# An encoder layer with mixture of experts: small items in two halves, token tiles moved between projections, last item behind the loops

## The chip, the cores and the metric

The kernel runs on one core of a Trainium2 chip. Its time is that of one whole execution on the device, in microseconds (us). TensorE is called PE in the profile (PEld: its weight loads, PEldq: its sequencer), VectorE is DVE, ScalarE is ACT, GpSimd is POOL, and SyncE is SP, which starts most DMA transfers.

## What is computed

One encoder layer on 1024 tokens of width 1024, all in float32. RMSNorm and one projection give queries, keys, values and a pooling input; differential attention and a pooling mixer follow, then an output projection. The second part is a mixture of experts: each token goes to 4 of 32 experts. At the end stands an RMSNorm over the whole row of each token:

```python
g = xb @ w_gate[e] + b_gate[e]
u = xb @ w_up[e] + b_up[e]
g = jnp.minimum(g, SWIGLU_LIMIT)
u = jnp.clip(u, -SWIGLU_LIMIT, SWIGLU_LIMIT)
act = (u + 1.0) * (g * jax.nn.sigmoid(g * SWIGLU_ALPHA))
y = act @ w_down[e] + b_down[e]
...
x = x + moe(rmsnorm(x, norm2[l]), ...)
return rmsnorm(x, final_norm)
```

## The kernel before

**Projections.** 32 products `proj_step` (L1161), numbered n, each with 8 steps over 128 rows of the weights. The first 16 need token tiles 0 to 3, the last 16 tiles 4 to 7. A tile reaches the projections in three steps: VectorE scales it (`scale_tokens`, L811), TensorE transposes it in 8 pieces (`transposes`, L1146), VectorE moves it out of PSUM (`move_hT`, L817). Tiles 4 to 7 take these steps in a row at n = 16.

**Items.** The rows of an expert are cut into items of at most 128; an item is treated as one of 32, 64, 96 or 128 rows. With these inputs there are 47: 24 of 128, 8 of 96, 7 of 64 and 8 of 32 rows, and each 32-row item is followed by a 128-row item of the same expert. TensorE jumps to the code of the item's size (`run_item`); the four pieces of code stand one behind the other in memory (32, 128, 64, 96). The other engines run one loop body for all sizes, `Fori(0, MAX_ITEMS)` with MAX_ITEMS = 64, of which 17 turns are empty.

An item works in units of 256 of the 1024 hidden columns. Where an item has under 128 rows, column groups of TensorE's array work side by side: with 32 rows four groups take one unit's share each, so that all 1024 hidden columns are one unit (b = 0), with N = 512 (256 gate and 256 up columns) in each product. The order of a 32-row item is: half of the gate and up products (`gate_up`, L1388, k = 0 to 3), the transposes of the next item's first rows (L1325), the other half (k = 4 to 7), the index products for a later item (`index`, L1317), register loads for the next item (`next_item`, L1487 to L1490), the transposes of the next item's other rows (L1325), the bias of the down projection (L1412), the transposes of the hidden rows (L1396), and the down projection (`down_32`, L1449). Between the gate and up products and L1396, ScalarE takes the sigmoid (L739) and VectorE does three steps (L1094, L1096, L1099); between L1396 and L1449, ScalarE moves the transposed rows (L743). 64-row items have two units and the down projection `down_64` (L1435) in four parts; there the second unit's hidden rows are transposed after the second part.

SyncE loads an expert's weights in four parts as the last item of the one before frees them: gate and up rows 0 to 3 and 4 to 7 (L408), down rows 0 to 3 and 4 to 7 (L415, semaphores `s_wk[2]` and `s_wk[3]`). The last of these is issued when the item before has ended.

**The end of an item and of the kernel.** ScalarE scales the item's rows by their gates (L759), GpSimd adds them to the residual rows in DRAM in four indirect transfers (L590). After the loops SyncE waits for the last item's addition, loads all 1024 rows (L451), ScalarE squares and sums them and takes a root (L767, L769), VectorE takes the reciprocal and scales (L1118, L1122), and SyncE stores (L455).

## Time and profile before

| | us |
|---|---|
| median of 3 runs | 2294.33 (2292.27 to 2297.32) |
| the profiled execution | 2295.37 |
| its span, first to last instruction | 2293.6 |
| TensorE busy | 2184.3 (95% of the span) |
| the chain that ended last: TensorE, DMA | 92%, 4% of the span |
| projections and pooling products | 15.5 to 251.4 |
| attention and output projection | to 548.3 |
| items | 579.35 to 2258.19 |
| after the last product | to 2293.6 |

The mean granted TensorE clock is 0.981 of full speed. A line number names a line of the kernel before. A timeline row has start, length, engine, line, operation, what it writes <- what it reads, count, and in brackets how long the engine had been idle and what ended it.

### The profile page before, as it was taken

The page shows a single profiled execution, that of the slowest core. Times are in us where ns is not written, and L with a number is a line of the kernel's source. Part 1 is how long each engine was busy: PE and PEld are TensorE (multiplying, and loading weights), DVE is VectorE, ACT ScalarE, POOL GpSimd, SP SyncE. Part 2 cuts the span into 40 slices and gives each one's busy share as a digit, 9 for nine tenths or more (in the row PEclk, how much of TensorE's full clock was granted, in tenths as well). Part 3 has the DMA queues.
Part 4 walks back from the last instruction along what each step waited for, and adds up shares of the span by engine and source line. Part 5 has one row for each costly group of instructions (what it writes and reads, how often), then busy time and mean ns, then how long its engine had stood idle before and what let it go on. Part 6 is the DMA issues. An engine that isn't in the chain of part 4 may idle for free.

```text
span 2293.6 us, 29668 instructions
## 1 busy us (share of the span) xinstructions
PE 2184.3 (95%) x9773; PEld 993.1 (43%) x9774; DVE 654.2 (29%) x1931; ACT 567.1 (25%) x1162; POOL 455.9 (20%) x480
## 2 busy tenths in 40 slices
PE   8999899997899999999999999999999999999993
PEld 4444477543444344344433434434443444444441
DVE  2010599354322222221222222222122212222223
ACT  2000488311221222211122222221122211222223
POOL 1014011214121212212122121221212211222121
PEclk9999999998999999999999999999999999999997
DMA  6100300324567967858869796685889777677854
GB/s 264 37 0 0 147 1 1 101 91 157 190 206 292 369 228 239 307 173 319 313 207 365 243 337 221 229 300 179 314 311 381 273 269 292 204 240 243 311 183 165
DMA packets 148233, 499.00 MB, mean 218 GB/s; under 512 B 10058, under 2 KB 34655, under 8 KB 146623
## 3 DMA queue, kind: packets, MB, share of 16 engines
q1 hardware_dynamic: 112192, 443.12, 50.1%
q0 software_dynamic: 34128, 50.35, 10.9%
q10 hardware_dynamic: 1874, 5.02, 0.6%
q8 instruction: 24, 0.39, 0.1%
q14 instruction: 15, 0.11, 0.0%
HBM read 460.15 MB, written 42.50 MB: 219 GB/s over the span
## 4 chain that ended last, share of the span: by engine, by line
PE 92%; DMA 4%; DVE 2%; issue 1%; POOL 1%; ACT 1%; SPq 0%; ACTq 0%; DVEq 0%; POOLq 0%
PE psum L1388 42%; PE psum L1424 14%; PE psum L1161 10%; PE psum L1216 5%; PE psum L1435 4%; PE psum L1234 3%; PE psum L1205 3%; PE psum L1449 3%; PE psum L1325 2%; DMA weights<-in_w_down 2%; PE psum L1396 2%; PE psum L1382 2%; PE psum L1243 1%; DMA weights<-in_w_up 1%; DMA work<-normed_rows,work 1%
## 5 line engine op out<-in xcount | busy, mean ns | idle before, releaser
L1388 PE MATMUL psum<-weights,work 128*128 128x512 f32 (+2 forms) x3520 | 1030.7, 599 | 1.7 <-DMA weights<-in_w_up 1.7
L1388 PEld LDWEIGHTS psum<-weights,work 128*128 128x128 f32 (+2 forms) x3520 | 381.0, 153 | 486.3 <-issue 477.8
L590 POOL DMA_INDIRECT residual_rows<-work x188 | 293.1, 1559 | 456.5 <-ACT work L759 410.4
L1424 PE MATMUL psum<-weights,work 128*128 128x512 f32 x768 | 337.5, 592 | 0.0
L1001 DVE TENSOR_REDUCE work<-psum 128x8 f32 x48 | 8.8, 184 | 803.1 <-PE psum L1339 803.1
L550 POOL DMA_INDIRECT work<-normed_rows,work x49 | 50.4, 1028 | 898.8 <-DVE work L988 840.4
L1161 PE MATMUL psum<-weights 128*128 128x512 f32 x512 | 220.5, 593 | 2.6 <-DVE weights L817 2.6
L1424 PEld LDWEIGHTS psum<-weights,work 128*128 128x128 f32 x768 | 143.9, 190 | 164.4 <-issue 160.8
L725 ACT ACTIVATE work<-psum 128x512 f32<-128x512 f32 x96 | 57.8, 602 | 445.9 <-PE psum L1325 445.9
L739 ACT ACTIVATE work<-psum 128x256 f32<-128x256 f32 x188 | 71.3, 384 | 382.5 <-PE psum L1388 382.5
L759 ACT ACTIVATE work<-psum,work 128x256 f32<-128x256 f32 x188 | 73.8, 476 | 334.0 <-PE psum L1424 239.5
L1094 DVE TENSOR_SCALAR work<-psum 128x256 f32<-128x256 f32 x188 | 79.7, 424 | 254.2 <-ACT work L739 247.1
L1161 PEld LDWEIGHTS psum<-weights 128*128 128x128 f32 x512 | 97.0, 190 | 125.0 <-issue 121.9
L1216 PE MATMUL psum<-weights 128*128 128x512 f32 x256 | 113.3, 600 | 0.0
L1435 PE MATMUL psum<-weights,work 128*64 128x512 f32 x480 | 109.3, 597 | 3.3 <-ACT work L743 3.3
L743 ACT ACTIVATE work<-psum 128x256 f32<-128x256 f32 x188 | 72.8, 387 | 159.3 <-PE psum L1396 159.3
L1099 DVE SCALAR_TENSOR_TENSOR work<-work 128x256 f32<-128x256 f32 x188 | 80.0, 426 | 19.5
L863 DVE CUSTOM_DVE_ANT_0 work<-psum,weights 128x1024 f32<-128x1024 f32 x64 | 78.4, 1225 | 12.0 <-PE psum L1205 11.9
L643 ACT ACTIVATE work<-work,negmax 128x1024 f32<-128x1024 f32 x64 | 73.3, 1145 | 31.0 <-DVE negmax L867 30.9
L1096 DVE TENSOR_TENSOR work<-psum,work 128x256 f32<-128x256 f32 x188 | 78.0, 415 | 0.0
L1396 PEld LDWEIGHTS psum<-ident,work 128*128 128x128 f32 x284 | 36.3, 141 | 91.0 <-issue 81.7
L1449 PE MATMUL psum<-weights,work 128*32 128x256 f32 x1024 | 65.3, 410 | 8.7 <-ACT work L743 4.4
(194 smaller groups left out, 1553.6 us busy)
## 6 DMA issues: line engine op xcount, KB each, us to landing
weights<-in_w_gate SPq DMA_DIRECT2D x64, 2048.0 KB, 7.9
weights<-in_w_up SPq DMA_DIRECT2D x64, 2048.0 KB, 13.7
weights<-in_w_down SPq DMA_DIRECT2D x64, 2048.0 KB, 11.4
weights<-in_w_in SPq DMA_DIRECT2D x8, 1024.0 KB, 16.4
residual_rows<-x SPq DMA_DIRECT2D x9, 512.0 KB, 3.8
normed_rows<-work ACTq DMA_DIRECT2D x9, 512.0 KB, 3.9
x<-in_x SPq DMA_DIRECT2D x8, 512.0 KB, 9.5
bias_rows_repeated<-bias_rows SPq DMA_DIRECT2D x4, 1024.0 KB, 10.2
```

The costliest lines, as they stand in the source:

```text
L590: pl.indirect_dma_start(acc_d[:, :], bass.IndirectOffsetOnAxis(dest[:, b:b + 1], 0), yrow[:, b * BLK:(b + 1) * BLK], None, compute_op=ALU. ...
L863: dve.tensor_tensor_reduce(out=prob[:, u % SETS, m, :], in0=PS[:, 2 * m * HALF:(2 * m + 2) * HALF], in1=bias[:, h, at:at + SEQ], scale=1.0 ...
L1094: dve.tensor_scalar(ucl[:, b, :], bank(b, BLK, BLK), LIMIT + 1.0, 1.0 - LIMIT, ALU.min, ALU.max).then_inc(s_ucl, 1)
L1096: dve.tensor_tensor(gact[:, b, :], bank(b, BLK), sig[:, b, :], ALU.mult).then_inc(s_sg, 1)
L1099: dve.scalar_tensor_tensor(hid[:, b, :], gact[:, b, :], ACT_LIMIT, ucl[:, b, :], ALU.min, ALU.mult).then_inc(s_hid, 1)
L1161: return pe.matmul(bank(4 + n % 4), lhs, rhs, start=(k == 0), stop=(k == DT - 1))
L1216: mm = pe.matmul(bank(n % 4), mixT[:, c, i * P:(i + 1) * P], w_out[:, c, q * HALF:(q + 1) * HALF], start=(c == 0), stop=(c == DT - 1))
L1388: mm = pe.matmul(out.rearrange("p (m n) -> p m n", m=2), xT[:, k, lo:lo + cols], wgu[:, :, k, blk * BLK:(blk + 1) * BLK], start=False, sto ...
L1396: mm = pe.transpose(bank(6, P, s * P), hid[:, b, s * P:(s + 1) * P], ident[:, :])
L1424: mm = pe.matmul(bank(4 + h), actT[:, k, :], wdn[:, k, h * HALF:(h + 1) * HALF], start=False, stop=(k == DT - 1))
L1435: mm = pe.matmul(PS[64 * h:64 * h + 64, 4 * HALF:5 * HALF], actT[:, 2 * b + s, 64 * c:64 * c + 64], wdn[:, k, h * HALF:(h + 1) * HALF], st ...
L1449: mm = pe.matmul(PS[32 * h:32 * h + 32, at:at + BLK], actT[:, 2 * b + s, 32 * c:32 * c + 32], wdn[:, k, h * BLK:(h + 1) * BLK], start=Fals ...
```

## The change

There are four parts.

First, a 32-row item has two units of 512 hidden columns, each with N = 256 products (128 gate and 128 up columns per group). The unit that was one becomes `gate_up_32(0)` and `gate_up_32(1)`; the hidden rows are transposed in two single pieces, the first before and the second within the down projection. `down_32(0)` uses down rows 0 to 3 and `down_32(1)` rows 4 to 7. Gate and up matrix instructions of such an item in the program go from 32 to 64, bias instructions from 4 to 8; all of its matrix instructions go from 98 to 134.

Second, in a 64-row item the transposes of the second unit's hidden rows stand one part of the down projection earlier.

Third, token tiles 4 to 7 are scaled, transposed and moved between the projections n = 5 to 13.

Fourth, the loops of ScalarE, VectorE and GpSimd end one item earlier and the last item stands behind them. The residual rows are loaded when the last but one item has been added, and squared, normalized and stored while the last item runs. The last item's tokens are then done again: GpSimd gathers their residual rows as 256-column pieces (`ylast`), VectorE adds, ScalarE squares, TensorE adds up the pieces of a token by three small products, GpSimd takes the power -0.5, VectorE scales, and GpSimd writes the pieces to the output by index. Roots are taken by GpSimd's power step instead of ScalarE's root and VectorE's reciprocal.

```diff
             sp.wait_ge(s_accin, 16 * (TT + 1))
-            sp.wait_ge(s_added, n_items + 1)
+            sp.wait_ge(s_added, n_items)
             for i in range(TT):
                 sp.dma_start(xv[:, i, :], acc_rows[i * P:(i + 1) * P, :]).then_inc(s_res[i], 16)
+            kind = sp.value_load(items[0:1, bass.ds(n_items + (2 * TABLE - 1), 1)], min_val=0, max_val=KINDS - 1)
+            sp.wait_ge(s_k03, n_items)
+            sp.dma_start(glast, t["last"][bass.ds(kind * P, P), :]).then_inc(s_glast, 16)
+            sp.dma_start(same.rearrange("p a c -> p (a c)"), t["same"]).then_inc(s_glast, 16)
             od = out[0].rearrange("(t p) d -> t p d", p=P)
             for i in range(TT):
                 sp.wait_ge(s_fo, i + 1)
-                sp.dma_start(od[i], fout[:, i % OUTS, :]).then_inc(s_out[i % OUTS], 16)
-            for b in range(OUTS):
-                sp.wait_ge(s_out[b], 16 * TT // OUTS)
+                sp.dma_start(od[i], xv[:, i, :]).then_inc(s_out, 16)
+            sp.wait_ge(s_out, 16 * TT)
+            sp.wait_ge(s_lout, 16 * UNIT)
...
-                with pl.If(j < n_items):
+                with pl.If(j < n_items - 1):
...
+            pl.wait_ge(s_k03, n_items)
+            pl.sem_inc(s_begin, 1)
+            pl.memset(lsq[:, UNIT:UNIT + 1], 1.0).then_inc(s_one, 1)
+            pl.wait_ge(s_dest, n_items + 1)
+            pl.sem_inc(s_begin, 1)
+            for b in range(UNIT):
+                pl.indirect_dma_start(ylast[:, b * BLK:(b + 1) * BLK], None, acc_d[:, :],
+                                      bass.IndirectOffsetOnAxis(dest[:, b:b + 1], 0)).then_inc(s_ylast, 16)
+            for lo, hi in ((0, 2), (2, 4), (4, 8)):
+                pl.wait_ge(s_fss, hi)
+                link(pl.tensor_scalar(fms[:, lo:hi], fsum[:, lo:hi], 1.0 / D, EPS, ALU.mult, ALU.add))
+                pl.tensor_tensor(frs[:, lo:hi], fms[:, lo:hi], halfneg[:, 0:hi - lo], ALU.pow).then_inc(s_frs, hi - lo)
+            pl.wait_ge(s_lms, 1)
+            pl.tensor_tensor(lrs, ltot, halfneg[:, :], ALU.pow).then_inc(s_lrs, 1)
+            pl.wait_ge(s_out, 16 * TT)
+            ob = out[0].rearrange("t (q n) -> (t q) n", q=UNIT)
+            for b in range(UNIT):
+                pl.wait_ge(s_lo, b + 1)
+                pl.indirect_dma_start(ob, bass.IndirectOffsetOnAxis(dest[:, b:b + 1], 0),
+                                      yrow[:, b * BLK:(b + 1) * BLK], None, bounds_check=UNIT * SEQ - 1,
+                                      oob_is_err=False).then_inc(s_lout, 16)
+            pl.wait_ge(s_lout, 16 * UNIT)
...
+            def square_rows(i):
+                act.wait_ge(s_res[i], 16)
+                if i:
+                    act.wait_ge(s_fss, i)
+                act.activation(fjunk, xv[:, i, :], ACT.Square, accum_out=fsum[:, i:i + 1]).then_inc(s_fss, 1)
...
+            last = act.value_load(total[0:1, 1:2], min_val=EXPERTS - 1, max_val=MAX_ITEMS - 1)
+            move_xT(n_items, 0)
+            sigmoid(last, 0)
+            sigmoid(last, 1)
+            move_hidden(last, 0)
+            sigmoid(last, 2)
+            move_hidden(last, 1)
+            act.wait_ge(s_k03, n_items)
+            square_rows(0)
+            square_rows(1)
+            sigmoid(last, 3)
+            move_hidden(last, 2)
+            move_xT(n_items, 1)
+            square_rows(2)
+            square_rows(3)
+            move_hidden(last, 3)
+            for i in range(4, TT):
+                square_rows(i)
+            act.wait_ge(s_fss, TT)
+            for b in range(UNIT):
+                act.wait_ge(s_fy, b + 1)
+                act.activation(fjunk[:, b * BLK:(b + 1) * BLK], yrow[:, b * BLK:(b + 1) * BLK], ACT.Square,
+                               accum_out=lsq[:, b:b + 1]).then_inc(s_lsq, 1)
...
+                    if 5 <= n <= 11:
+                        if n > 5:
+                            move_hT((n + 1) // 2)
+                        scale_tokens((n + 3) // 2)
                     if n == 13:
-                        scale_tokens(4)
+                        move_hT(TT - 1)
 
             scale_tokens(0)
             for i in range(4):
@@ -836,10 +900,6 @@
                     scale_tokens(i + 1)
                 move_hT(i)
             proj_moves(0)
-            for i in range(4, TT):
-                if i < TT - 1:
-                    scale_tokens(i + 1)
-                move_hT(i)
             proj_moves(1)
...
+            last = dve.value_load(total[0:1, 1:2], min_val=EXPERTS - 1, max_val=MAX_ITEMS - 1)
+            dve.wait_ge(s_rps, n_items + 1)
+            dve.sem_inc(s_found, 1)
+            unit(last, 0)
+            unit(last, 1)
+            dve.wait_ge(s_added, n_items)
+            dve.tensor_copy(dest, nextitem[:, 0:4]).then_inc(s_ldve, 1)
+            dve.tensor_copy(dgate, nextitem[:, 4:8]).then_inc(s_ldve, 1)
+            dve.wait_ge(s_ldve, 2)
+            dve.sem_inc(s_dest, 1)
+            unit(last, 2)
+            unit(last, 3)
             dve.wait_ge(s_gfin, 16)
             for i in range(TT):
-                dve.wait_ge(s_frms, i + 1)
-                dve.reciprocal(frs[:, i:i + 1], frms[:, i:i + 1]).then_inc(s_frs, 1)
                 dve.wait_ge(s_frs, i + 1)
-                if i >= OUTS:
-                    dve.wait_ge(s_out[i % OUTS], 16 * (i // OUTS))
-                dve.scalar_tensor_tensor(fout[:, i % OUTS, :], xv[:, i, :], frs[:, i:i + 1], gfin, ALU.mult,
+                dve.scalar_tensor_tensor(xv[:, i, :], xv[:, i, :], frs[:, i:i + 1], gfin, ALU.mult,
                                          ALU.mult).then_inc(s_fo, 1)
+
+            dve.wait_ge(s_dps, n_items)
+            dve.wait_ge(s_ylast, 16 * UNIT)
+            for b in range(UNIT):
+                dve.scalar_tensor_tensor(yrow[:, b * BLK:(b + 1) * BLK], bank(4 + b // 2, BLK, (b % 2) * BLK),
+                                         dgate[:, b:b + 1], ylast[:, b * BLK:(b + 1) * BLK], ALU.mult,
+                                         ALU.add).then_inc(s_fy, 1)
+            dve.wait_ge(s_glast, 32)
+            dve.wait_ge(s_ltps, 1)
+            dve.tensor_tensor(lprod, bank(7, 3 * (UNIT + 1)).unsqueeze(1).to_broadcast([P, UNIT, 3 * (UNIT + 1)]), share,
+                              ALU.mult).then_inc(s_ldve, 1)
+            dve.wait_ge(s_ldve, 3)
+            dve.tensor_reduce(ltot, lprod, AX_X, ALU.add).then_inc(s_lms, 1)
+            dve.wait_ge(s_lrs, 1)
+            for b in range(UNIT):
+                dve.scalar_tensor_tensor(yrow[:, b * BLK:(b + 1) * BLK], yrow[:, b * BLK:(b + 1) * BLK], lrs[:, b:b + 1],
+                                         glast[:, b * BLK:(b + 1) * BLK], ALU.mult, ALU.mult).then_inc(s_lo, 1)
...
+                if n in (7, 9, 11, 13):
+                    transposes((n + 1) // 2)
                 if n == 16:
-                    for i in range(4, TT):
-                        transposes(i)
                     pe.wait_ge(s_hT, 16)
...
+                def gate_up_32(b, ks):
+                    for c in range(4):
+                        out = PS[32 * c:32 * c + 32, b * HALF:(b + 1) * HALF].rearrange("p (m n) -> p m n", m=2)[:, :, 0:P]
+                        at = b * HALF + c * P
+                        if ks[0] == 0:
+                            pe.matmul(out, chosen[0:3 * EXPERTS, 0:32], bgu[:, :, at:at + P], start=True, stop=False)
+                    for k in ks:
+                        for c in range(4):
+                            out = PS[32 * c:32 * c + 32, b * HALF:(b + 1) * HALF].rearrange("p (m n) -> p m n", m=2)[:, :, 0:P]
+                            at = b * HALF + c * P
+                            mm = pe.matmul(out, xT[:, k, 0:32], wgu[:, :, k, at:at + P], start=False, stop=(k == DT - 1))
+                    return mm
+
                 def gate_up(b, ks):
+                    if tokens == 32:
+                        return gate_up_32(b, ks)
...
+                def down_32(b, blocks=range(4)):
+                    pe.wait_ge(s_aTm, UNIT * j + b + 2)
+                    pe.wait_ge(s_wk[2 + b], 16 * e + 16)
+                    for c in blocks:
+                        for h in range(4):
+                            mm = pe.matmul(PS[32 * h:32 * h + 32, 4 * HALF:4 * HALF + BLK],
+                                           actT[:, 2 * b, 32 * c:32 * c + 32],
+                                           wdn[:, 4 * b + c, h * BLK:(h + 1) * BLK], start=False,
+                                           stop=(4 * b + c == DT - 1))
+                    return mm
+
+                units = 2 if tokens == 32 else {64: 2, 96: 3, 128: 4}[tokens]
...
                 if tokens == 32:
                     gate_up_ends(0)
+                    gate_up_ends(1)
                     next_item()
+                    hidden(0)
                     rows(1)
                     down_bias()
-                    hidden(0)
-                    down_32(0).then_inc(s_dps, 1)
+                    down_32(0, range(0, 2))
+                    hidden(1)
+                    down_32(0, range(2, 4)).then_inc(s_d03, 1)
+                    down_32(1).then_inc(s_dps, 1)
...
                     down_64(0, 0)
+                    hidden(1)
                     down_64(0, 1)
-                    hidden(1)
                     down_64(1, 0).then_inc(s_d03, 1)
...
+            pe.wait_ge(s_glast, 32)
+            pe.wait_ge(s_one, 1)
+            pe.wait_ge(s_lsq, UNIT)
+            for n, lhs in enumerate((ident[:, :], same[:, 0, :], same[:, 1, :])):
+                mm = pe.matmul(bank(7, UNIT + 1, n * (UNIT + 1)), lhs, lsq, start=True, stop=True)
+            mm.then_inc(s_ltps, 1)
```

TensorE at the projections, before. Each L1161 row counts products, 8 to a projection.

```order
L1146 MATMUL psum<-ident,work 128x128 x32
L1161 MATMUL psum<-weights 128x512 x32
L1174 MATMUL psum<-work 4x512 x4
L1161 MATMUL psum<-weights 128x512 x96
L1146 MATMUL psum<-ident,work 128x128 x32
L1161 MATMUL psum<-weights 128x512 x128
```

The same stretch after the change (L1236 are the transposes, L1251 the products).

```order
L1236 MATMUL psum<-ident,work 128x128 x32
L1251 MATMUL psum<-weights 128x512 x32
L1264 MATMUL psum<-work 4x512 x4
L1251 MATMUL psum<-weights 128x512 x24
L1236 MATMUL psum<-ident,work 128x128 x8
L1251 MATMUL psum<-weights 128x512 x16
L1236 MATMUL psum<-ident,work 128x128 x8
L1251 MATMUL psum<-weights 128x512 x16
L1236 MATMUL psum<-ident,work 128x128 x8
L1251 MATMUL psum<-weights 128x512 x16
L1236 MATMUL psum<-ident,work 128x128 x8
L1251 MATMUL psum<-weights 128x512 x152
```

The transposes of tiles 4 to 7 stood in one piece of 32 between projections 15 and 16; they now stand in four pieces of 8 before projections 7, 9, 11 and 13.

TensorE in a 32-row item, from the register loads (which stand right ahead) to the end, before (L1325 transposes of the next item's rows, L1412 bias, L1396 hidden rows, L1449 down products).

```order
L1471 REGISTER_ALU
L1325 MATMUL psum<-ident,work 128x128 x4
L1400 REGISTER_ALU
L1412 MATMUL psum<-work 32x256 x4
L1393 REGISTER_ALU
L1396 MATMUL psum<-ident,work 128x128 x2
L1442 REGISTER_ALU
L1445 ISA
L1449 MATMUL psum<-weights,work 32x256 x32
```

The same after the change, again behind the register loads (L1501 hidden rows, L1415 next item's rows, L1517 bias, L1564 down products).

```order
L1501 MATMUL psum<-ident,work 128x128
L1585 REGISTER_ALU
L1415 MATMUL psum<-ident,work 128x128 x4
L1505 REGISTER_ALU
L1517 MATMUL psum<-work 32x256 x4
L1561 ISA
L1564 MATMUL psum<-weights,work 32x256 x8
L1498 REGISTER_ALU
L1501 MATMUL psum<-ident,work 128x128
L1564 MATMUL psum<-weights,work 32x256 x8
L1560 REGISTER_ALU
L1564 MATMUL psum<-weights,work 32x256 x16
```

One pair of transposes before one run of 32 products became single transposes before runs of 8 and of 24.

ScalarE in the last item, behind the loop (L777 sigmoid, L781 moves of hidden rows, L788 squares of residual rows, L829 squares of the item's rows).

```order
L776 REGISTER_ALU
L777 ACTIVATE work<-psum 128x256
L781 ACTIVATE work<-psum 128x256
L788 ACTIVATE weights<-x 128x1024 x2
L776 REGISTER_ALU
L777 ACTIVATE work<-psum 128x256
L781 ACTIVATE work<-psum 128x256
L763 REGISTER_ALU
L764 ACTIVATE work<-psum 128x512
L788 ACTIVATE weights<-x 128x1024 x2
L781 ACTIVATE work<-psum 128x256
L788 ACTIVATE weights<-x 128x1024 x4
```

The squares that stood after the last item now stand in four places of it, with no table load between sigmoids and squares.

## Rows read from the trace of the kernel before

**Rows 1.** The chain that ended last, in order of time (start us, us)
```profile
15.51 27.73 PE psum L1161 x64
```

**Rows 2.** Waits of TensorE (us in total, times, longest us)
```profile
PE psum L1396 <- DVE work L1099: 7.7, 8, 1.0
...
PE psum L1449 <- ACT work L743: 4.4, 8, 0.6
PE psum L1449 <- DMA weights<-in_w_down: 4.3, 2, 3.4
PE psum L1435 <- ACT work L743: 3.3, 7, 0.5
```

**Rows 3.** Busy time by stretch, between the two halves of the projections
```profile
core 0: us, PE busy (x) PEld busy (x) DVE busy (x) ACT busy (x) POOL busy (x), PEclk, DMA share, GB/s
...
126.65:134.36 7.71, 4.31 (x33) 3.37 (x31) 7.46 (x12) 0.00 (x0) 0.00 (x0) 1.00 0.00 1
```

**Rows 4.** The same view: two of the eight 32-row items
```profile
857.11:871.92 14.81, 13.28 (x164) 5.51 (x163) 6.41 (x25) 7.65 (x16) 6.23 (x4) 1.00 0.85 283
...
1428.13:1444.57 16.44, 14.91 (x163) 6.23 (x163) 7.61 (x29) 7.65 (x16) 7.14 (x5) 0.90 0.77 257
```

**Rows 5.** Timeline of TensorE in a 32-row item (start us, us)
```profile
861.66 3.64 PE L1388 MATMUL psum<-weights,work 128*32 128x512 f32 x32
865.24 0.35 PE L1317 MATMUL psum<-work 128*128 x8
...
867.28 0.44 PE L1396 MATMUL psum<-ident,work 128*128 128x128 f32 x2 [0.97 <-DVE work L1099]
868.28 3.66 PE L1449 MATMUL psum<-weights,work 128*32 128x256 f32 x64 [0.56 <-ACT work L743]
```

**Rows 6.** TensorE's sequencer, L1317 and L1490 (ns min/median/max)
```profile
L1317 PEldq FUSED_REGOPS  x8: 46/46/65, 862.8 to 863.7; - x8
...
L1490 PEldq TENSOR_LOAD <-work x1: 297/297/297, 864.9 to 864.9; - x1
```

**Rows 7.** Timeline of TensorE, a place where weights come last
```profile
809.02 3.26 PE L1449 MATMUL psum<-weights,work 128*32 128x256 f32 x32 [3.38 <-DMA weights<-in_w_down]
```

**Rows 8.** SyncE and transfers, 2029 to 2046 us (last: landing)
```profile
2031.06 0.37 SPq L415 DMA_DIRECT2D weights<-in_w_down  x1
...
weights<-in_w_down SPq DMA_DIRECT2D x1, 2048.0 KB, 10.9
```

**Rows 9.** DMA queues of 570 to 800 us, then of 800 to 2280
```profile
q8 instruction: 7, 0.11, 0.2%
...
q0 software_dynamic: 30095, 43.53, 14.7%
```

**Rows 10.** Timeline of all engines after the last item
```profile
2258.19 1.57 ACT L759 ACTIVATE work<-psum,work 128x256 f32<-128x256 f32 x4 [9.98 <-PE psum L1424]
...
2265.84 1.28 ACT L767 ACT_TABLE_LOAD   x1 [6.08 <-issue]
2266.14 1.55 POOL L590 DMA_INDIRECT residual_rows<-work  x1 [0.30 <-issue]
2270.10 3.95 SPq L451 DMA_DIRECT2D x<-residual_rows  x8
2273.85 1.06 ACT L767 ACTIVATE weights<-x 128x1024 f32<-128x1024 f32 x1 [6.73 <-DMA x<-residual_rows]
...
2276.91 1.28 DVE L1122 SCALAR_TENSOR_TENSOR weights<-x,weights,work 128x1024 f32<-128x1024 f32 x1
...
2278.22 12.11 SPq L455 DMA_DIRECT2D out_rows<-weights  x8
```

**Rows 11.** Timeline of ScalarE in the last item
```profile
2247.83 0.38 ACT L743 ACTIVATE work<-psum 128x256 f32<-128x256 f32 x1 [3.49 <-PE psum L1396]
```

**Rows 12.** Groups by line: two kinds of GpSimd instruction
```profile
L550 POOL DMA_INDIRECT work<-normed_rows,work x49 | 50.4, 1028 | 898.8 <-DVE work L988 840.4 <-issue 57.4 <-POOL work L563 1.0
...
L480 POOL TENSOR_TENSOR rstd<-meansq,halfneg 128x1 f32<-128x1 f32 x16 | 11.9, 745 | 1.3
```

146 lines of the change are left out of this document (80 added, 66 removed).

## Prediction

> **What bounds the kernel now.** I read the chain that ended last first. TensorE carries 92% of it and DMA 4% (the table), so outside the end of the kernel only what shortens TensorE's path pays. Its pieces also give the price of full-speed work: 64 matrix rows of N = 512 in 27.73 us, 0.43 us each [rows 1]. Next, the waits of TensorE in the items: 7.7 us before the hidden transposes of the eight 32-row items, 4.4 us before their down projection, 3.3 us in the seven 64-row items, 4.3 us for down weights [rows 2]. Then the stretch between the halves of the projections: 7.71 us, TensorE busy for 4.31 [rows 3]. Last, the end: the last product is over when L759 starts at 2258.19, the span ends at 2293.6, and TensorE does nothing in these 35.4 us [rows 10].
>
> **Projections.** The same 32 transposes and the same vector steps remain. What goes is TensorE's idle time, 7.71 - 4.31 = 3.4 us [rows 3]. The new places wait for nothing: VectorE scales and moves one tile (some 2 us) for every second projection, and two take some 14 us. The banks of the transposes (0 to 3) are not those of the projections (4 to 7), and tile 7 is moved two projections before n = 16 asks for it. **Gain 3.4 us**, bounds 2.8 (the four switches cost 0.15 us each, below) and 3.5.
>
> **64-row items.** The wait of 0.47 us stands between the second unit's transposes and its down products, while ScalarE moves the rows. Afterwards a part of the down projection lies between them, four products in two pairs side by side, each of two passes of 0.43 us [rows 1], so 1.7 us, which covers it. The hidden rows are ready, since transposes of two units, bias and a first part lie ahead. Two of the seven (at 1228 and 1731 us) are followed by waits for weights, where time saved is waited again. 5 x 0.47 = **2.3 us**, bounds 1.5 and 3.3.
>
> **32-row items.** Undisturbed, one lasts 14.81 us [rows 4], with idle stretches of 0.97 and 0.56 us [rows 5]. Both are one unit's path through ScalarE and VectorE. I follow the new order from the start of the second half of gate and up, t. The row of 32 at N = 512 lasts 3.58 us to the next start (861.66 to 865.24); the 64 at N = 256 of L1449 last 3.66 [rows 5], so halving N costs next to nothing and a unit's half lasts 1.8 us. But the sequencer matters now. It sends eight index products from 862.8 and has the last register load behind it at 865.2, 2.4 us later [rows 6], which today ends just as TensorE needs it. Afterwards it has sent unit 0 at about t + 1.0 (64 instructions, as the 64 of today), index at 2.1, unit 1 at 3.1, and with the rest of those 2.4 us, 1.4 for the register loads, reaches the hidden transposes at t + 4.6. TensorE finishes unit 1 at t + 3.95, so a gap of about 0.65 us is new. Then 0.14 (one transpose), 0.56 (next rows), 0.15 (bias), 0.9 (two of the eight down blocks) give t + 6.3; unit 1's hidden rows are ready at t + 3.95 + 2.0 = 5.95, the 2.0 being today's way from 865.24 to 867.28. Transpose, two blocks, and the last four: t + 9.1; unit 1's move by ScalarE, about 0.9 us as today from 867.28 to 868.28 less one transpose, is hidden under two blocks. Today the same point is 868.28 + 3.66 - 861.66 = t + 10.3. That is 1.2 us; I take off 0.15 for one more switch between 32-column and full-width work: **1.0 us per item**, bounds 0.3 and 1.6 (all idle time gone).
>
> On switches: the half of 8 passes at 0.43 us [rows 1] would last 3.43 and lasts 3.58 with a switch in and out [rows 5], so a pair costs 0.15 us. The Trainium skill, TensorEngine Tiling (Array Packing), section Key Properties, says that changing the tiling mode drains TensorE; this speaks against cutting the runs, as the change does in two more places. The row shows the drain but at 0.15 us, and the sum goes by that.
>
> Six of eight gain. At 792.55 and at 1253.43 the last quarter of the down weights decides: at 809.02 TensorE had waited 3.38 us for it [rows 7], and the later half of the down projection still stands behind it. The closest of the six is at 2030.96: weights issued at 2031.06 land 10.9 us later, 2042.0 [rows 8]; half of the down projection is reached near 2043.9 now and 1.0 us earlier then. It fits by 0.9 us. 6 x 1.0 = **6.0 us**.
>
> Three of the six (at 1428, 2090, 2196 us) last 16.4 us at a mean granted clock of 0.90, where others last 14.8 at 1.00 [rows 4]: the clock fell to 1.2 GHz around the down projection, after 1.53 us idle in two pieces. The 64-row items with 0.47 us idle kept 2.4 GHz seven times of seven. With a gap of 0.65 I expect it kept: 3 x 1.6 = **4.8 us**, bounds 0 and 4.8. Items of 96 and 128 rows do the same work in the same order: 0.
>
> **The end.** In the last item ScalarE, VectorE and GpSimd each turn 18 empty loops after item 46 (6.08 us for 17 today, before L767's table load [rows 10]), which the 15 us of first-half products cover. Residual rows are in SBUF long before ScalarE asks. The squares of rows 0 to 3 fit into ScalarE's idle time. The path that sets the end, in today's times: last hidden move over at 2248.2 [rows 11]; four squares of 1.06 + 0.19 to 2253.2; GpSimd's power step (0.75 [rows 12], with the scaling and hand-overs 1.2) to 2254.4; four row scalings of 1.28 [rows 10] to 2259.6, 1.4 us behind TensorE; four additions of 256 columns, 0.45 each, to 2261.5; square, three small products, two vector steps and the power step, 3.4 together, to 2264.9; first scaling, 2265.5. Stores of rows are then down: the last starts at 2259.7 and takes some 4.3. Four indirect writes begin 1.87 us apart as today's additions do, the last at 2271.1, and land 3.96 us later (today 2266.14 to 2270.10 [rows 10]): 2275.1, against 2293.6. **Gain 18.5 us.** Bounds: writes as cheap as the gather L550 (1.03 instead of 1.55 [rows 12]) and shorter hand-overs, 22; late stores or 0.5 us more at each of eight hand-overs, 14.5.
>
> **Sum.** 3.4 + 2.3 + 6.0 + 4.8 + 18.5 = 35.0 us. The profiled execution took 2295.37, 1.8 us around its span of 2293.6, and 1.04 above the median. 2295.4 - 35.0 = 2260.4, less 1.0: **2259.4 us**. Bounds together: 2251 and 2273; not all ends meet.
>
> **Rivals.**
> *The clock still falls.* The new gap of 0.65 us plus waits at the hidden rows could do what 1.53 us do. It stays then in three items: 2259.4 + 4.8 = 2264. For it: the fall came in three of six items with equal idle times, so small shifts decide. Against: the 64-row items.
> *The 32-row items do not gain.* The register loads keep their 1.4 us and the unit path hides elsewhere; the item stays at 14.8 or 16.4 us, 10.8 us lost from the sum: 2270. The change would then not do what it says there. Against: two idle stretches of today lie on one unit's path, which half a unit covers.
> *The end is tighter.* Two vector passes, 0.6 us behind in GpSimd's queue (four gathers stand ahead of the first power step) or a store that lands after 2265.5 put 4 us on it: 2263.5.
> *The end is cheaper* (plain writes as cheap as gathers): 2255.
> *Slower: the code of the items no longer stays on the core.* From 570 to 800 us seven packets of instructions (16 KB each) came in on TensorE's queue, while each size ran for the first time; from 800 to 2280 us there is none [rows 9], though TensorE jumped between the sizes forty times. So all four pieces of code are held. The 32-row piece grows from 98 to 134 matrix instructions in the program, some 37% more rows than its 327 [rows 4], 120. Seven packets came in for about 1400 rows and some 150 control instructions, so a packet holds about 220: the code grows by half a packet. If what is held ends just there, a piece is fetched anew whenever it is wanted: I estimate the time of a gather's start, 1 to 2 us, at each of 46 items, up to 92 us: 2351. It decides where the loop reaches into one more packet than is held. Against: half a packet reaches the next one only every other time, and nothing shows that the store was full.
> The Trainium skill, Runtime: NRT & Kernel Launch, section Instruction fetch mechanics, says that a taken branch to a target outside a window of two pages must fetch it first. By that rule every item would fetch today; the trace shows no packet in 1480 us.
>
> **Chances.** Forecast 0.52; clock falls 0.13; no gain in 32-row items 0.06; tighter end 0.13; cheaper end 0.12; slower 0.04. What this kernel's measurement can tell from no change is 0.2%, 4.6 us. All cases but the last lie over 24 us below 2294.33. Range: from the cheaper end and full gains, 2252, to the clock's fall and part of a tighter end, 2267; 0.17 is left out. Faster 0.95, same 0.01, slower 0.04.
>
> **What would show it.** 32-row items of 13.7 us and a clock of 1.00 in them; 64-row items of 24.3; four groups of eight transposes without idle time between projections; residual squares between sigmoids in the last item, and 17 us from the last down product to the end. Wrong would be: instruction packets on TensorE's queue after 800 us; idle time before the hidden transposes over 1 us; a last store of whole rows that lands after the last item's first scaling.

## The result, and the profile after

The changed kernel takes **2261.63 us** (median of four runs, 2259.18 to 2266.84) against 2295.15 (four runs of before beside them, 2292.27 to 2297.32): a ratio of 0.9859, 95% interval 0.9845 to 0.9872. The forecast was 2259.4, range 2252 to 2267. Run again later beside other runs of before, it had a ratio of 0.9867 (0.9843 to 0.9891).

The profiled execution took 2263.67 us with a span of 2261.8, against 2295.37 and 2293.6. The 31.8 us between the spans divide as follows (starts and ends of products read from the timelines; the first product itself starts 0.2 us later after):

| stretch, us | before | after | gained | forecast |
|---|---|---|---|---|
| projections, first to last product | 229.0 | 224.7 | 4.3 | 3.4 |
| from there to the first item | 334.9 | 334.6 | 0.3 | 0 |
| 64-row items 2, 16, 22, 34, 38 | 5 x 24.74 | 5 x 24.20 | 2.7 | 2.3 |
| 32-row items 0, 8, 24, 40, 42, 45 | 96.8 | 88.2 | 8.6 | 10.8 |
| the rest, where weights come last (6 with 7, 18 with 19, 32) | 139.0 | 140.8 | -1.7 | 0 |
| last down product to the end | 35.5 | 17.7 | 17.8 | 18.5 |

The projections, after. The timeline of TensorE (start us, us, engine, line, operation, count): the line of the 32 transposes is L1236, that of the projections L1251.

```profile
65.02 1.04 PE L1236 MATMUL psum<-ident,work 128*128 128x128 f32 x8
65.90 13.90 PE L1251 MATMUL psum<-weights 128*128 128x512 f32 x32
79.63 1.04 PE L1236 MATMUL psum<-ident,work 128*128 128x128 f32 x8
80.51 13.90 PE L1251 MATMUL psum<-weights 128*128 128x512 f32 x32
```

No row has an idle time in brackets, and the next product starts 0.88 us after the first of eight transposes (65.02 to 65.90, 79.63 to 80.51). Four such groups cost 3.5 us; the stretch of [rows 3] cost 7.71.

The 32-row items, by stretch (columns as in [rows 3]). The first two answer to the two of [rows 4], the third is the item whose weights come last.

```profile
851.80:865.96 14.16, 13.69 (x232) 7.50 (x231) 6.05 (x22) 7.75 (x16) 6.23 (x4) 1.00 0.88 292
1422.39:1436.63 14.24, 13.76 (x231) 7.51 (x231) 6.09 (x22) 7.75 (x16) 6.23 (x4) 1.00 0.88 295
1246.35:1272.46 26.11, 17.20 (x232) 8.59 (x230) 8.57 (x30) 7.85 (x16) 7.23 (x5) 0.80 0.93 331
```

Idle time of TensorE fell from 14.81 - 13.28 = 1.53 us to 14.16 - 13.69 = 0.47, but its busy time rose from 13.28 to 13.69. In the second item the granted clock is 1.00 where it was 0.90.

Waits of TensorE after, which answer to [rows 2]:

```profile
PE psum L1564 <- DMA weights<-in_w_down: 6.8, 2, 4.1
...
PE psum L1475 <- DMA weights<-in_w_up: 4.1, 1, 4.1
...
PE psum L1501 <- DVE work L1144: 2.3, 5, 0.5
PE psum L1487 <- DMA weights<-in_w_up: 1.2, 1, 1.2
PE psum L1501 <- issue: 1.0, 3, 0.5
```

The waits for ScalarE before down products (4.4 and 3.3 us in [rows 2]) are gone, those before the hidden transposes (L1501, 7.7 before) are down to 3.3. The waits for weights have grown, for w_down from 4.3 to 6.8 us and for w_up from 2.4 to 5.3. The rows for w_up before:

```profile
PE psum L1388 <- DMA weights<-in_w_up: 1.7, 1, 1.7
...
PE psum L1382 <- DMA weights<-in_w_up: 0.7, 1, 0.7
```

The end after, in the timeline of all engines; last down product over at 2244.09:

```profile
2233.82 0.38 ACT L781 ACTIVATE work<-psum 128x256 f32<-128x256 f32 x1 [1.21 <-PE psum L1501]
...
2239.40 1.01 POOL L625 TENSOR_TENSOR weights<-weights,halfneg 128x4 f32<-128x4 f32 x1
2240.44 4.87 DVE L1195 SCALAR_TENSOR_TENSOR x<-x,weights,work 128x1024 f32<-128x1024 f32 x4 [3.86 <-POOL weights L625]
2245.23 1.65 DVE L1201 SCALAR_TENSOR_TENSOR work<-psum,work,weights 128x256 f32<-128x256 f32 x4
...
2249.25 1.01 POOL L627 TENSOR_TENSOR weights<-weights,halfneg 128x4 f32<-128x4 f32 x1 [8.84 <-DVE weights L1209]
2250.29 1.67 DVE L1212 SCALAR_TENSOR_TENSOR work<-work,weights 128x256 f32<-128x256 f32 x4 [1.12 <-POOL weights L627]
2251.71 1.21 POOL L632 DMA_INDIRECT out_rows<-work  x1 [1.46 <-DVE work L1212]
2253.22 0.98 POOL L632 DMA_INDIRECT out_rows<-work  x1 [0.30 <-issue]
...
2255.79 0.98 POOL L632 DMA_INDIRECT out_rows<-work  x1 [0.31 <-issue]
```

Set 14.0 us later (2258.09 - 2244.09), this is the forecast's list to 0.3 us up to the first write: last hidden move over 2248.2 (2248.2), row scalings over 2259.3 (2259.6), first write 2265.7 (2265.5). The last write starts 1.3 us sooner than forecast, 2269.8 (2271.1). What follows the last write is in the section on the end.

### The profile page after: what moved, and what is told of

It is laid out like the page before. It is cut to its first block, busy times and chain, and to the rows that moved or that the text cites. A ratio compares the mean times of both kernels' runs of the same rounds, so it can differ in the third digit from the quotient of the medians.

```text
span 2261.8 us, 30785 instructions
## 1 busy us (share of the span) xinstructions
PE 2183.6 (97%) x10323; PEld 1010.8 (45%) x10324; DVE 652.2 (29%) x1919; ACT 563.0 (25%) x1156; POOL 461.3 (20%) x490
## 3 DMA queue, kind: packets, MB, share of 16 engines
q0 software_dynamic: 33792, 50.35, 10.8%
## 4 chain that ended last, share of the span: by engine, by line
PE 93%; DMA 3%; DVE 1%; POOL 1%; issue 1%; ACT 1%; ACTq 0%; DVEq 0%; SPq 0%; POOLq 0%
PE psum L1493 41%; PE psum L1529 14%; PE psum L1251 10%; PE psum L1306 5%; PE psum L1540 4%; PE psum L1324 3%; PE psum L1295 3%; PE psum L1415 2%; DMA weights<-in_w_down 2%; PE psum L1501 2%; PE psum L1487 2%; PE psum L1475 1%; PE psum L1552 1%; PE psum L1564 1%; PE psum L1333 1%
## 5 line engine op out<-in xcount | busy, mean ns | idle before, releaser
L1493 PE MATMUL psum<-weights,work 128*128 128x512 f32 (+2 forms) x3008 | 969.0, 594 | 0.0
L1493 PEld LDWEIGHTS psum<-weights,work 128*128 128x128 f32 (+2 forms) x3008 | 365.6, 159 | 449.8 <-issue 443.8
L605 POOL DMA_INDIRECT residual_rows<-work x184 | 286.6, 1558 | 447.3 <-ACT work L805 400.9
L565 POOL DMA_INDIRECT work<-normed_rows,work x48 | 49.3, 1028 | 861.4 <-DVE work L1048 802.9
L1251 PE MATMUL psum<-weights 128*128 128x512 f32 x512 | 220.9, 593 | 1.3 <-DVE weights L877 1.3
L777 ACT ACTIVATE work<-psum 128x256 f32<-128x256 f32 x188 | 71.9, 383 | 385.8 <-PE psum L1493 362.1
L1251 PEld LDWEIGHTS psum<-weights 128*128 128x128 f32 x512 | 96.9, 190 | 121.9 <-issue 120.3
L781 ACT ACTIVATE work<-psum 128x256 f32<-128x256 f32 x188 | 72.4, 385 | 141.7 <-PE psum L1501 141.6
L1144 DVE SCALAR_TENSOR_TENSOR work<-work 128x256 f32<-128x256 f32 x188 | 80.0, 425 | 25.8 <-DVE work L1141 11.0
L1501 PEld LDWEIGHTS psum<-ident,work 128*128 128x128 f32 x284 | 36.9, 141 | 92.1 <-issue 86.0
L1306 PEld LDWEIGHTS psum<-weights 128*128 128x128 f32 x256 | 48.5, 193 | 57.8 <-issue 57.8
```

The costliest lines, as they stand in the source:

```text
L605: pl.indirect_dma_start(acc_d[:, :], bass.IndirectOffsetOnAxis(dest[:, b:b + 1], 0), yrow[:, b * BLK:(b + 1) * BLK], None, compute_op=ALU. ...
L1144: dve.scalar_tensor_tensor(hid[:, b, :], gact[:, b, :], ACT_LIMIT, ucl[:, b, :], ALU.min, ALU.mult).then_inc(s_hid, 1)
L1251: return pe.matmul(bank(4 + n % 4), lhs, rhs, start=(k == 0), stop=(k == DT - 1))
L1306: mm = pe.matmul(bank(n % 4), mixT[:, c, i * P:(i + 1) * P], w_out[:, c, q * HALF:(q + 1) * HALF], start=(c == 0), stop=(c == DT - 1))
L1493: mm = pe.matmul(out.rearrange("p (m n) -> p m n", m=2), xT[:, k, lo:lo + cols], wgu[:, :, k, blk * BLK:(blk + 1) * BLK], start=False, sto ...
L1501: mm = pe.transpose(bank(6, P, s * P), hid[:, b, s * P:(s + 1) * P], ident[:, :])
```

## Experiments: one part at a time

Four kernels are the kernel before with one part of the diff each.

**The projections alone**: the lines of the diff in `proj_moves` and in TensorE's loop over n, nothing else.

```diff
+                if n in (7, 9, 11, 13):
+                    transposes((n + 1) // 2)
                 if n == 16:
-                    for i in range(4, TT):
-                        transposes(i)
```

> The kernel before with one part of the change: token tiles 4 to 7 are transposed and moved between the projections. Theory (the prediction's first step): all 32 items and all vector steps stay, only the 3.4 us of idle time go; 2294.3 - 3.4 = 2290.9 us, the first item starts 3.4 us sooner, and the items keep their lengths. What it tells apart besides: the three 32-row items at 1428, 2090 and 2196 us lasted 16.4 us before because the clock fell in them. If the idle time inside these items makes it fall, all three stay at 16.4 us here. If where they lie in time decides, a shift by 3.4 us moves the falls to other items or takes them away, up to 4.8 us more.

Measured: 2291.77 us, ratio 0.9977 (0.9968 to 0.9986), so 5.3 us less by the ratio, 3.2 to 7.3. From the first to the last projection product it took 224.7 us as in the changed kernel, 4.3 less. The clock fits neither picture in full: the items are 3.4 us earlier, the three long ones stay long, and **a fourth** 32-row item is long now, that at 2028.54, which lasted 14.75 before. With a first item that is 1.5 us longer as well, this one profiled execution has the same span as before, 2293.6 us; the gain shows in the median of ten runs.

```profile
2028.54:2045.11 16.57, 14.92 (x164) 6.23 (x164) 7.62 (x29) 7.64 (x16) 7.18 (x5) 0.90 0.75 250
```

**The 32-row items alone**: `gate_up_32`, `down_32`, `down_rest` and the order for `tokens == 32`, nothing else.

```diff
                     gate_up_ends(0)
+                    gate_up_ends(1)
                     next_item()
+                    hidden(0)
                     rows(1)
                     down_bias()
-                    hidden(0)
-                    down_32(0).then_inc(s_dps, 1)
+                    down_32(0, range(0, 2))
+                    hidden(1)
...
```

> The kernel before with one part of the change: the 32-row items in two units of 512 hidden columns, nothing else. From the two traces at hand I expect 14.2 us per undisturbed item (0.6 less than 14.8, where the prediction had 1.0 less), six times, so 3.6 us, and the three falls of the clock gone, 4.8 us; item 7 longer by 0.8 us as in the changed kernel: some 8 us, 2286 us. Theory A, the idle time inside the item makes the clock fall: all three items at 14.2 us. Theory B, the place in time decides: one or more of them stays near 16 us, and the gain is 4 to 6 us.

Measured: 2290.62 us, ratio 0.9970 (0.9957 to 0.9984), 6.9 us less, 3.7 to 9.9. Items 8, 24, 40, 42 and 45 last 14.1 to 14.3 us, and none shows a fall of the clock. Items 18 and 19 together last 50.5 us, 1.6 longer than before (below).

**The 64-row line alone**:

```diff
                     down_64(0, 0)
-                    down_64(0, 1)
                     hidden(1)
+                    down_64(0, 1)
```

> The kernel before with one line moved: in 64-row items the second unit's hidden transposes stand before the second part of the down projection. Theory: the wait of 0.47 us for ScalarE goes in seven items, 0.54 us by the lengths in the two traces; in the items at 1228 and 1731 us it comes back as a wait for weights: 5 x 0.54 = 2.7 us, 2291.6 us. Rival: the later down weights (the quarter that the first part does not need) decide somewhere, then less than 2 us.

Measured: 2295.76 us, ratio 0.9998 (0.9989 to 1.0007). Six of the seven items last 24.20 us instead of 24.74 (the seventh waits for weights), so the wait went as expected. By the runs the gain is 0.5 us, with 2.5 as its upper bound, so the expected 2.7 lies just outside: that the 0.54 us per item reach the kernel's time is not shown here. The first item began 1.2 us later than in the profile of before; its start scatters from one execution to the next (579.4 to 581.3 us in the four kernels with the old projections). Four kernels with the old 32-row order give this count of long ones among the items 24, 40, 42 and 45: before 3, projections alone 4, this one 1 (at 2088.68), the end alone 1 (the last). The idle time does not tell them apart. In this run the items at 1428.52 and 2088.68 both waited 1.11 to 1.12 and 0.56 us before the same products, and only the second lost the clock:

```profile
1428.52:1443.46 14.94, 13.27 (x164) 5.50 (x163) 6.40 (x25) 7.65 (x16) 6.24 (x4) 1.00 0.84 280
2088.68:2105.27 16.59, 14.92 (x163) 5.88 (x163) 7.62 (x29) 7.65 (x16) 7.16 (x5) 0.90 0.76 252
```

**The end alone**: everything of the diff behind the loops, with the loops one item shorter.

```diff
-                with act.If(j < n_items):
+                with act.If(j < n_items - 1):
```

> The kernel before with one part of the change: the last item behind the loops and the new end. The prediction had 18.5 us for it, the two traces show 17.8 from the last down product to the end of the span. So 2294.3 - 17.8 = 2276.5 us. If the parts add up, this and the other three together give the 33 to 34 us of the whole change; if the end is worth less alone, it was paid by the items ahead of it. Items before the last keep their lengths, the three falls of the clock stay.

Measured: 2277.85 us, ratio 0.9918 (0.9905 to 0.9932), 18.8 us less, 15.6 to 21.8. From the last down product to the end 17.5 us. The four together give 31.5 us, the whole change 32.4 (0.9859): the parts add up within their intervals.

## Experiments: what stands before the hidden transposes

In the changed kernel 0.48 us of idle time are left in a 32-row item. The forecast had laid such a gap to the register loads in TensorE's sequencer; the waits name VectorE. Its timeline in the profile after (L1407 index products, L1055 VectorE reads the index, L1144 ends unit 0, L1501 hidden transposes):

```profile
2191.32 0.42 PE L1407 MATMUL psum<-work 128*128 x8
...
2192.44 0.16 DVE L1055 CAST work<-psum 128x6 bf16<-128x6 f32 x1 [2.02 <-PE psum L1407]
...
2194.09 0.33 PE L1501 MATMUL psum<-ident,work 128*128 128x128 f32 x1 [0.48 <-DVE work L1144]
```

**Register loads later**, behind the down bias:

```diff
                     gate_up_ends(1)
-                    next_item()
                     hidden(0)
                     rows(1)
                     down_bias()
+                    next_item()
```

> The changed kernel, but in 32-row items the register loads for the next item stand behind the down bias instead of before the first hidden transposes. Theory B (the prediction's: these 1.4 us of loads make the gap before the hidden transposes): the gap of 0.48 us goes, the item lasts 13.7 us. Theory A (VectorE makes it): the gap stays at 0.48, the item lasts 14.2 us or up to 0.5 more, since the loads now stand before the down products.

Measured (one run and its profile, 2266.9 us): items of 15.0 us.

```profile
2196.54 0.33 PE L1501 MATMUL psum<-ident,work 128*128 128x128 f32 x1 [0.48 <-DVE work L1144]
...
2198.35 1.07 PE L1564 MATMUL psum<-weights,work 128*32 128x256 f32 x16 [0.82 <-issue]
```

The gap of 0.48 stays, so here VectorE makes it. A new one of 0.82 stands where the loads are now: they do hold TensorE when nothing is queued behind them.

**Index products behind both units**, in bank 5, read by VectorE before unit 2:

```diff
-                    if b == 0:
+                    if b == (1 if tokens == 32 else 0):
                         pe.wait_ge(s_found, j + 2)
-                        index(j + 2, bass.ds(e2, 1)).then_inc(s_ips, 1)
+                        pe.wait_ge(s_yr, UNIT * j + UNIT)
+                        index(j + 2, bass.ds(e2, 1), at=5).then_inc(s_ips, 1)
```

> The changed kernel, but the index products of the item after next no longer stand between the two units of a 32-row item: they come behind both, go to bank 5 instead of 6, and VectorE reads them before its third unit instead of before its first. What it tells apart: in the changed kernel 0.48 us of idle time stand before the first hidden transposes of each 32-row item. Theory A: VectorE is held, since it reads the index before unit 0, and the index's semaphore arrives 1.1 us after the first index product; then the first hidden transposes come 4.2 us after the start of the second half instead of 4.64, the item lasts 13.7 to 13.8 us instead of 14.2, six times 0.45, in all 2.7 us: 2259 us. Theory B (the prediction's): the loads of registers behind unit 1 hold TensorE's sequencer; they stand in the same place here, so the gap stays and the item lasts 14.2.

Measured: 2275.94 us, ratio 0.9912 (0.9898 to 0.9925), slower than the changed kernel. Two waits appear:

```profile
PE psum L1502 <- issue: 8.4, 8, 1.2
PE psum L1515 <- DVE work L1055: 8.1, 7, 1.2
```

The second is a fault of the edit: the down bias was made to wait for the read of the index, which in 64-row items comes only before unit 2; 1.2 us seven times. The first is the question asked: the transposes (L1502) wait for nothing but the sequencer, up to 1.2 us, since index and register loads now stand in a row with no products queued behind them. So the sequencer makes the gap here, which is theory B's cause but not its number: the item is 14.55 us long instead of 14.2, with a gap of 1.1 to 1.2 us. There are two chains, VectorE's and the sequencer's, and the order decides which is last.

**The changed kernel once more** gave the other half:

> The changed kernel itself, beside the next two on the same chip: 2261.6 us as before. The falls of the clock inside the 32-row items at 1429, 2022, 2081 and 2185 us stay away if the new order of the item keeps the clock up; if it was luck of one execution, one or two of them come back (the old order showed nine in sixteen items at these four places over four kernels).

Measured: 2261.98 us, ratio 0.9867 (0.9843 to 0.9891). No long 32-row item. But in its profile VectorE reads the index 0.46 us after its first product, not 1.12, and the transposes come no sooner:

```profile
2189.41 0.42 PE L1407 MATMUL psum<-work 128*128 x8
...
2189.87 0.16 DVE L1055 CAST work<-psum 128x6 bf16<-128x6 f32 x1 [1.37 <-PE psum L1407]
2191.04 0.50 DVE L1144 SCALAR_TENSOR_TENSOR work<-work 128x256 f32<-128x256 f32 x1
...
2192.13 0.30 PE L1501 MATMUL psum<-ident,work 128*128 128x128 f32 x1 [0.44 <-issue]
```

VectorE is done at 2191.54, the products of unit 1 end at 2191.69, and TensorE waits 0.44 us for "issue". The last register load of this item is in the sequencer's own rows (ns, count, start):

```profile
L1604 PEldq TENSOR_LOAD <-work x1: 592/592/592, 2191.3 to 2191.3; - x1
```

It ends at 2191.9, and the transposes follow. In this execution the register loads make the gap, as in the forecast. But this load takes 0.59 us, where the same load in the first profile of the changed kernel took 0.33. In all five items without other waits (8, 24, 40, 42, 45) it took 0.50 to 0.59. Why is open. The 0.26 us more are over half of this gap, and the forecast did not have them. With prompt reads the item lasts 14.0 us, with late ones 14.2.

**Both chains shortened** (with the edits of the end, below): index products between the units as before but in bank 5, read before unit 1, and the down bias waits for this read; the third register load behind the last down products.

```diff
-                        if b == 0:
+                        if b == 1:
                             dve.wait_ge(s_ips, j + 3)
                             index_parts(j + 2)
```

> The changed kernel with the end of the run a_end and three edits in the items: the index products stay between the two units but go to bank 5, so that VectorE can read them before unit 1 instead of before unit 0; the third register load of a 32-row item (the expert after next) stands behind its last down products; the down bias waits for the read of the index. The earlier runs say that two chains end within 0.1 to 0.3 us of each other before the first hidden transposes: VectorE's, held by the index (9.2 us after the item's start), and the sequencer's with its three loads (8.9 to 9.1). Theory A: with both shortened, the transposes start when unit 1's products end, 8.75 instead of 9.21, the item lasts 13.7 to 13.8 us instead of 14.2; six times 0.45 = 2.7, with 2.3 from the end 5.0 us below the run beside it, 2256.6 us. Theory B: the late semaphores are TensorE's true times, it is busy until then, and the transposes stay at 9.2: 2.3 us from the end alone, 2259.3. If the moved load costs, the next item starts late by some 0.4 us.

Measured: 2262.88 us, ratio 0.9864 (0.9842 to 0.9887), the same as the changed kernel beside it (0.9867), though it has the shorter end too.

```profile
2196.16 0.33 PE L1501 MATMUL psum<-ident,work 128*128 128x128 f32 x1
...
2201.61 0.39 PE L1487 MATMUL psum<-work 96*128 96x512 bf16 x1 [0.46 <-issue]
```

The item began at 2187.39: the transposes come at 8.77, the gap is gone, theory A. And all of it is given back at the start of the next item, 0.46 us of "issue": the branches to the next item are sent behind the load that was moved.

**The load before the second hidden transposes instead**:

```diff
                     down_32(0, range(0, 2))
+                    third_item()
                     hidden(1)
                     down_32(0, range(2, 4)).then_inc(s_d03, 1)
                     down_32(1).then_inc(s_dps, 1)
-                    third_item()
```

> The run a_best with one line moved: in a 32-row item the third register load stands before the second hidden transposes instead of behind the last down products. In a_best the first hidden transposes came at 8.77 us after the start of the item, as its theory A says, but the next item began 0.46 us after the last product, since its instructions are sent behind that load. Before the second hidden transposes the sequencer waits for VectorE for 0.78 us (from 9.87 to 10.65), and the load takes 0.45. Theory A, there the load is free: transposes at 8.77, no idle time at the next item's start, the item lasts 13.8 us (14.0 to 14.2 in the two traces of the changed kernel), some 1.5 us in all six, and 2.5 from the end: a ratio to before of 0.984 where the changed kernel had 0.986 to 0.987. Theory B, the sequencer then is late for the last six blocks of the down projection: idle time of 0.2 us or more before them, and the item stays at 14.0 to 14.2.

Measured: 2260.28 us, ratio 0.9838 (0.9824 to 0.9851); items of 14.3 us.

```profile
2198.05 0.33 PE L1501 MATMUL psum<-ident,work 128*128 128x128 f32 x1
...
2198.76 0.38 ACT L776 ACTIVATE work<-psum 128x256 f32<-128x256 f32 x1 [2.32 <-PE psum L1475]
2199.04 0.38 ACT L780 ACTIVATE work<-psum 128x256 f32<-128x256 f32 x1
...
2199.55 1.07 PE L1565 MATMUL psum<-weights,work 128*32 128x256 f32 x16 [0.52 <-ACT work L780]
...
2203.59 0.39 PE L1487 MATMUL psum<-work 96*128 96x512 bf16 x1
```

The load is free now and the next item starts without idle time. But unit 1's products end at 2198.12, ScalarE's sigmoid of them (L776) is released only at 2198.76, and the move of unit 0's hidden rows (L780), for which the down products wait, stands behind it in ScalarE's queue. Neither theory had this third chain. That the item would reach 13.8 us is not shown. What delays such releases by some 0.65 us stays open, also because the profile's ends of products are modelled. In 32-row items of the new order they were late in six profiles (in two of these not in every item) and prompt in three, late in the changed kernel's first profile and prompt in its second.

## Experiments: the clock

**A longer gap**: three dependent copies on VectorE before unit 0.

```diff
+                        if b == 0:
+                            for n in range(3):
+                                chain(dve.tensor_copy(gact[:, 3, :], ucl[:, 3, :]))
                         unit(j, b)
```

> The changed kernel with three copies of 256 columns added on VectorE before unit 0 of every item, one behind the other: some 1.4 us. Only 32-row items have no cover for it, so that their gap before the first hidden transposes grows from 0.48 to about 1.9 us. Theory A, idle time inside the item makes the clock fall: in one to four of the six items (at 858, 1429, 2028, 2088, 2191 us and the first) it falls, those last some 17.2 us, the others 15.6; 6 x 1.4 = 8.4 us, and up to 6 more: 2270 to 2277 us. Theory B, one gap does not do it whatever its length, it was the pair of gaps before hidden transposes and down products: no fall, 15.6 us each, 2270 us.

Measured: 2268.65 us, ratio 0.9882 (0.9866 to 0.9897). The copies took some 0.35 us each, so the gap is 1.5, not 1.9:

```profile
2198.86 0.33 PE L1504 MATMUL psum<-ident,work 128*128 128x128 f32 x1 [1.52 <-DVE work L1144]
```

All of 8, 24, 40, 42 and 45 last 15.1 to 15.2 us, none with a fall. The old order had 1.5 to 1.7 us idle, in two pieces of 0.93 to 1.12 and 0.56, and the clock fell in nine of sixteen of the items 24, 40, 42 and 45. In the new order it fell in none of 36 (the same four items in nine profiles), with up to 1.5 us idle. The kernel with doubled code (below) has the new order too and is not among the nine: there the clock fell in all four, three of which waited 2.6 to 3.2 us for instructions. Theory A is refuted as far as the amount goes. Theory B, the pair, has a witness against it too: the run with the later register loads had gaps of 0.48 and 0.82 us, the second right before the down products, and no fall in its four items. Since only four items speak there, and the old order let seven of sixteen pass, that is weak. What of the new order keeps the clock up stays open; that it does so, where such longer waits are absent, is shown.

The price does not vanish either. Where weights come last the new order waits in one piece. Item 19, TensorE's timeline after:

```profile
1257.26 3.64 PE L1475 MATMUL psum<-weights,work 128*32 128x256 f32 x32 [4.10 <-DMA weights<-in_w_up]
...
1269.32 3.21 PE L1564 MATMUL psum<-weights,work 128*32 128x256 f32 x32 [2.64 <-DMA weights<-in_w_down]
```

The last down weights arrive 47.0 to 47.4 us after the start of item 18 in twelve profiles, old order or new (47.6 with the late index products, where item 18 itself is 0.7 us longer than before): transfers set this stretch, and 0.54 us saved in item 18 are waited again, as the forecast said. The 32 products behind them take 1.9 us at full clock in four profiles of the old order and four of the new, but 3.2 to 3.6 us here and in four more of the new order, because the clock fell in the wait or within 0.5 us behind it. Those five waited 2.1 to 2.8 us, the four without a fall 2.2, 2.3, 2.8 and 2.8; the old order waited 0.6 to 2.0 us there and kept the clock. So the length of the wait alone does not decide here either. In the second profile of the changed kernel items 18 and 19 took 49.3 us, without this fall, and 50.3 in the first.

## Experiments: the end

```diff
-            for lo, hi in ((0, 2), (2, 4), (4, 8)):
+            for lo, hi in ((0, 2), (2, 4), (4, 6), (6, 8)):
...
                                       oob_is_err=False).then_inc(s_lout, 16)
-            pl.wait_ge(s_lout, 16 * UNIT)
```

> The changed kernel with two edits at its end. First, GpSimd's third power step, for rows 4 to 7, is cut in two: rows 4 and 5 can be scaled while ScalarE squares 6 and 7. In the changed kernel the last row scaling ends 1.2 us after the last down product; here VectorE should be done at 2243, before the last product, and the additions start right behind it: 1.1 us. Second, GpSimd no longer waits for its last writes (SyncE still does): in the changed kernel its closing drain of 3.1 us starts when they have landed, and ends the span. Theory A, the drain is a fixed time of its own: it starts with the last issue and 1.5 us go, together 2.6 us, 2259 us. Theory B, the drain waits for the writes and then takes its 3.1 us: only 1.1 us go.

Measured: 2258.85 us, ratio 0.9840 (0.9826 to 0.9854), 15.4 us from the last down product to the end instead of 17.7. After a last instruction each engine runs a closing drain of its own. GpSimd's in the changed kernel (ns, start):

```profile
L65 POOLq DRAIN  x1: 3137/3137/3137, 2258.4 to 2258.4; - x1
```

and in this one, where GpSimd no longer waits for its writes:

```profile
L65 POOLq DRAIN  x1: 6740/6740/6740, 2254.9 to 2254.9; - x1
```

It ends at 2261.62. The last write was issued from 2257.50 to 2258.47 and landed at 2259.9; 3.14 us after the issue is 2261.61, while theory B would give 2263.0. **Theory A**: the drain ends a fixed time behind the last issue and may overlap the landing; in all three kernels without the wait this time is 3.14 or 3.15 us. It gives 1.6 of the 2.3 us; the power step cut in two gives some 0.65 (last down product to the end of the last issue, 12.68 and 12.03 us), not the 1.1 expected. In the kernel before the drain was 2.89 us long and started at 2278.1, hidden behind the stores.

## Experiment: the slower rival

```diff
+            with here("experts_half"):
+                pe.br_lt(copy, 1, on_true="experts_some", on_false="experts_some_b")
...
+            for tokens in (32, 128, 64, 96):
+                run_item(tokens, "_b")
```

> The changed kernel with the code of its four item sizes twice in the program; the two copies take turns, item by item, so that TensorE goes through twice as much code. Tests the slower rival: before and after, no packet of instructions came in on TensorE's queue from 800 us to the last item. Theory A, what is held is much more than four pieces: some seven packets more while the second copies run for the first time, none later, 2262 to 2266 us. Theory B, four pieces nearly fill it: packets in every item to the end, 1 to 2 us each, 46 to 92 us, 2310 to 2350 us.

Measured (one run and its profile): **2483.0 us**, 221 more than the changed kernel beside it. TensorE's instruction queue from 800 to 2400 us (132 packets by the end of the items at 2463), and TensorE's waits from 800 to 2460 us:

```profile
q8 instruction: 125, 2.05, 0.6%
```

```profile
PE psum L1487 <- issue: 121.6, 26, 12.9
```

Theory B, and at 4.8 us per item (221 / 46) instead of 1 to 2. The last three 32-row items last 23.7 to 23.8 us instead of 14.0, items 16 and 22 with 64 rows 31.8 instead of 24.2; TensorE's mean granted clock falls to 0.95 on top, so part of the 4.8 us is clock. In the changed kernel the same view shows no packet on q8 after 800 us, and seven from 570 to 800, as in [rows 9]. So the danger was real, and the change did not reach it: over the whole execution 24 packets came in on this queue, before and after. The Trainium skill, Runtime: NRT & Kernel Launch, section Instruction fetch mechanics, gives TensorE a store of 128 KiB filled in blocks of 16 KiB: seven blocks would fit, fourteen not. The trace agrees with that size: seven packets came in and stayed, with the code doubled they came again and again. The same section's window of two pages for branches does not describe what these rows show.

## Why the prediction was right, point by point

- **Projections, 3.4 us (bounds 2.8 and 3.5): 4.3.** The mechanism was right, the term too small. I took the 4.31 us busy of [rows 3] as what the transposes cost anywhere; between products eight of them cost 0.88 us, 3.5 in all, since the first overlaps the product ahead. The rest is the idle time, 7.71 - 3.5 = 4.2.
- **64-row items, 5 x 0.47: 5 x 0.54**, and the two that were to gain nothing gained nothing.
- **32-row items, 1.0 us each (0.3 to 1.6): 0.65, 0.55 and 0.81** in the three that had no fall of the clock around the down projection before (8, 40, and 0, which runs partly at 1.2 GHz in both profiles). The step that failed is the sum of the path, t + 9.1; it was t + 9.7 (2189.45 to 2199.14). No piece is far off: the two halves took 3.86 instead of 3.6, the bias 0.3 instead of 0.15, the second hidden transpose with its switches 0.25 instead of 0.14, the down blocks a little more each. A check was at hand in [rows 4]: idle time 1.53 us could only fall to the 0.65 that I kept, and busy time rose by my 0.15 at least, which leaves 0.73, not 1.0. Measured: idle 1.06 less, busy 0.41 more. TensorE's busy time is the mis-sized term, and the rows of item 8 show where, first before, then after:

```profile
857.11 0.40 PE L1382 MATMUL psum<-work 96*32 96x512 bf16 x4
...
860.88 0.35 PE L1339 MATMUL psum<-work 128*128 128x24 bf16 x8
...
865.45 0.63 PE L1325 MATMUL psum<-ident,work 128*128 128x128 f32 x4
```

```profile
851.80 0.29 PE L1470 MATMUL psum<-work 96*32 96x256 bf16 x4
...
855.59 0.35 PE L1429 MATMUL psum<-work 128*128 128x24 bf16 x8
...
856.37 1.93 PE L1475 MATMUL psum<-weights,work 128*32 128x256 f32 x32
858.24 0.42 PE L1407 MATMUL psum<-work 128*128 x8
858.59 1.94 PE L1475 MATMUL psum<-weights,work 128*32 128x256 f32 x32
```

  Halving N cost next to nothing, as forecast: the first half, which is not cut, took 3.77 us before and 3.79 after. The second half, which the index products cut in two, took 3.79 with them (from 861.66, [rows 5], to 865.45) and now takes 4.16 (856.37 to 860.53). These 0.37 us are most of the 0.41; the forecast had 0.15 for the one more run of 32-column work.
- **The gap of 0.65 by the register loads: 0.48 by VectorE in one execution, 0.44 by the loads in another.** The forecast did not look at VectorE's read of the index here. That the size is near is in part luck: in the second execution 0.26 us of the gap come from a load that took 0.59 us instead of 0.33.
- **The clock, 4.8 us: gone in all three**, as forecast, and in 36 of 36. But the size of 4.8 us was luck of one profile: nine falls in four profiles are 2.25 per execution, 3.6 us, not 4.8. The 0.13 for "the clock still falls" was too much for the reason given (amount of idle time).
- **Items with weights last, 0: -1.7.** Transfers set their ends, right; that a longer wait in one piece can cost clock afterwards (1.3 us in items 18 and 19 in this profile, 0.3 in the second one; some 0.4 in 6 and 7, where the fall at 804 us now reaches into item 7) was not in the sum.
- **The end, 18.5 (14.5 to 22): 17.8.** The steps hold to 0.3 us up to the first write. Two errors cancel behind it: the writes came 1.3 to 1.5 apart, not 1.87, and landed after 2.4, not 3.96, together 3.1 us less; but GpSimd became the last engine, and its drain of 3.1 us with 0.4 around it, hidden before, was forgotten.
- **Rivals.** "Tighter" and "cheaper" end were both partly true and cancelled. "Instructions no longer held" did not come true; its mechanism is real, and some three times as dear as I wrote. The lower end of the bounds together adds up to 2274, not 2273; nothing hangs on it.
- The sum in the trace was 35.0 against 31.8 measured; the medians lie nearer, since the profiled execution after was 2.0 us above its median, where before's was 1.0.

**A better version?** The kernel with the two edits of the end has a ratio to before of 0.9840, those with item edits too 0.9864 and 0.9838, the changed kernel 0.9859 and 0.9867. By the traces the end is 2.1 to 2.9 us shorter in all three, but one of them, run beside the changed kernel, is no faster than it, and the intervals overlap. So a shorter end is shown, a faster kernel is not, and for the item edits nothing is shown.

## What to carry to other kernels

When a path is re-laid piece by piece, check the sum against a balance of the stretch: what of the idle time can go at most, and what busy time is added by more and smaller instructions. A gap that is filled has a second chain right behind it: look at VectorE's, ScalarE's and the sequencer's ends before you count the whole gap, and use waits of the sequencer as the free place for register loads. And ask which engine will be the last one to finish, since it brings its closing drain along; a wait that another engine keeps need not be kept twice.

## What the runs showed of the hardware

- TensorE went through four pieces of code (seven packets of 16 KB when first run) for 1400 us without a fetch; twice the code cost 4.8 us per item, lost clock included.
- Eight 128 x 128 transposes between products of N = 512 cost 0.88 us from the first to the next product, not the 1.1 they last when each group is waited for.
- 64 matrix rows of N = 256 in place of 32 of N = 512 took the same time, with their bias (3.79 and 3.77 us); a run of 32-column work cut in two by the full-width index products cost 0.37 us.
- A register load in TensorE's sequencer mostly takes 0.30 to 0.33 us, in 32-row items at times up to 0.59, and with its address step and the spaces some 0.45. Three in a row take some 1.4 us; where no products were queued behind them TensorE waited 0.8 to 1.2 us.
- GpSimd's closing drain is 2.9 to 3.1 us; where nothing waits for the last write, it ends 3.14 us behind the issue of that write and overlaps the landing.
- In some executions VectorE and ScalarE start some 0.65 us late on TensorE's products in the 32-row items (L1055 1.12 us after the index products' start instead of 0.46); open why.
- The clock fell in nine of sixteen items with 1.5 to 1.7 us idle in two pieces (16.4 to 16.6 us instead of 14.8 to 14.9), and in none of 36 in the new order of the same work with up to 1.5 us idle.
